# A hybrid attention step on one core: keys and queries of mixer A projected and normed during mixer B, index dots block by block

## The reference

```python
xn = rms_norm(x, norm_g)
h = einsum('btd,de->bte', xn, w_in)
qa, ka, va, ua, qi, ki, wi, qb, kb, vb, ub, ga, gb = split(h)
qa, ka = rope(rms_norm(qa, q_norm_g)), rope(rms_norm(ka, k_norm_g))   # per head
qi, ki = rope(qi), rope(rms_norm(ki, idx_k_norm_g))
# mixer A: index scores, top 128 keys (72 for the samples), softmax over them
dots  = einsum('bqhd,bsd->bqhs', qi, ki) * 64 ** -0.5
score = einsum('bqhs,bqh->bqs', relu(dots), wi)      # masked to the admissible keys
oa = softmax(qa . ka[top_k(score)] * 64 ** -0.5) . va[top_k(score)]
# mixer B: stick breaking, strictly causal
z  = einsum('bqhd,bshd->bhqs', qb, kb) * 64 ** -0.5
ob = (exp(log_sigmoid(z) + sum of log_sigmoid(-z) behind the key)) . vb
y  = x + (sigmoid(ga) * (oa * silu(ua)) @ w_a_out + sigmoid(gb) * (ob * silu(ub)) @ w_b_out) @ w_o
```

## Time and profile before

| | us |
|---|---|
| median of the runs | 573.23 |
| time of the profiled execution | 572.14 |
| its span, first to last instruction | 570.4 |
| PE busy in the span | 539.1 |
| DVE, ACT, POOL busy | 323.1, 222.4, 76.4 |
| mean granted TensorE clock | 0.973 of full speed |

### The profile page before, as it was taken

How to read it: one execution, slowest core, us unless ns; L and a number is a source line. 1 busy time by engine, 2 the same in 40 slices (tenths; PEclk the granted TensorE clock), 3 DMA queues, 4 the chain that set the end, 5 groups by cost and what they waited for, 6 DMA issues and landing times.

```text
span 570.4 us, 10220 instructions
## 1 busy us (share of the span) xinstructions
PE 539.1 (95%) x4344; PEld 511.8 (90%) x4344; DVE 323.1 (57%) x650; ACT 222.4 (39%) x354; POOL 76.4 (13%) x87
## 2 busy tenths in 40 slices
PE   4999699999999999989969799999999999999998
PEld 3889699999999999979969788898899999999997
DVE  5805647788987886734763456663245433456331
ACT  7614645215445456423403666643413323123110
POOL 4313000001342222160450000000000000000000
PEclk9999989999999999987979899999899999999999
DMA  8611202541102220240422005021033222227311
GB/s 329 239 74 38 85 1 74 183 160 64 51 37 76 75 75 1 75 148 1 153 74 75 2 1 180 22 75 38 1 111 111 75 60 90 75 94 280 140 49 50
DMA packets 15214, 50.45 MB, mean 88 GB/s; under 512 B 2400, under 2 KB 5856, under 8 KB 11584
## 3 DMA queue, kind: packets, MB, share of 16 engines
q1 hardware_dynamic: 15168, 49.79, 24.7%
HBM read 42.82 MB, written 6.82 MB: 87 GB/s over the span
## 4 chain that ended last, share of the span: by engine, by line
PE 86%; DVE 5%; POOL 3%; ACT 3%; issue 2%; DMA 1%; SPq 0%; ACTq 0%; DVEq 0%
PE PS L506 34%; PE PS L723 13%; PE PS L784 9%; PE PS L766 8%; PE PS L460 4%; PE PS L638 4%; PE PS L617 3%; PE PS L492 3%; POOL nrs L1584 2%; PE PS L561 2%; PE PS L593 2%; PE PS L701 2%; ACT whi L830 1%; PE PS L454 1%; DVE wlo L1111 1%
## 5 line engine op out<-in xcount | busy, mean ns | idle before, releaser
L506 PE MATMUL PS<-xhi,whi 128*128 128x272 f32 x320 | 94.9, 297 | 5.7 <-DVE q_flat L1216 5.3
L1111 DVE TENSOR_TENSOR wlo<-raw,whi 128x2048 fp32r<-128x2048 f32 (+1 forms) x36 | 74.4, 2068 | 36.0 <-ACT whi L830 35.9
L506 PE MATMUL PS<-xlo,whi 128*128 128x272 f32 x320 | 93.2, 291 | 0.0
L506 PE MATMUL PS<-xhi,wlo 128*128 128x272 f32 x320 | 92.7, 290 | 0.0
L830 ACT ACTIVATE whi<-raw 128x2048 fp32r<-128x2048 f32 (+1 forms) x36 | 61.7, 1718 | 76.8 <-PE PS L723 33.7
L506 PE MATMUL PS<-whi,xhi 128*128 128x256 f32 x256 | 77.3, 302 | 3.9 <-DVE oT L1304 3.3
L506 PE MATMUL PS<-wlo,xhi 128*128 128x256 f32 x256 | 75.3, 294 | 0.0
L506 PE MATMUL PS<-whi,xlo 128*128 128x256 f32 x256 | 74.7, 292 | 0.0
L506 PEld LDWEIGHTS PS<-xhi,whi 128*128 128x128 f32 x320 | 60.9, 190 | 9.3 <-DVE q_flat L1216 5.6
L506 PEld LDWEIGHTS PS<-xhi,wlo 128*128 128x128 f32 x320 | 61.0, 191 | 0.0
L506 PEld LDWEIGHTS PS<-xlo,whi 128*128 128x128 f32 x320 | 60.9, 190 | 0.0
(11 more groups left out here) (204 smaller groups left out, 1135.2 us busy)
## 6 DMA issues: line engine op xcount, KB each, us to landing
raw<-in_w_units SPq DMA_DIRECT2D x28, 1024.0 KB, 4.9
stage<-in_x_kw_qi SPq DMA_DIRECT2D x8, 564.0 KB, 7.2
raw<-in_w_mixes SPq DMA_DIRECT2D x8, 512.0 KB, 3.5
res<-in_x_kw_qi SPq DMA_DIRECT2D x1, 2176.0 KB, 8.0
out<-res SPq DMA_DIRECT2D x16, 136.0 KB, 1.7
out<-vals SPq DMA_DIRECT2D x2, 1024.0 KB, 5.4
out<-kT SPq DMA_DIRECT2D x1, 1088.0 KB, 6.5
out<-tm SPq DMA_DIRECT2D x1, 1024.0 KB, 4.3
```

The costliest lines, as they stand in the source:

```text
L506: mm = pe.matmul(out, lhsT, rhs, start=(k == 0), stop=(k == 23))
L1111: dve.tensor_tensor(wlo[:, uu % 2, 0:n], raw[:, uu % 2, 0:n], whi[:, uu % 2, 0:n].bitcast(F32), ALU.subtract).then_inc(w_lo, 1)
```

## The change

- `UNITS`: `ub0` goes ahead of `kb0`; `ka0` and `ka1` go ahead of `ub1`. The loads on SP follow, and the store of A's new keys moves ahead of the load of `ua1`.
- Four groups of `vb1` stand ahead of the dots. The dots go block by block (3, 2, 1, "s"), eight heads each, with a group after every fourth dot. From block 2 on DVE makes a round of top-k on block 3 after every second dot. `topk_half` now takes the two blocks that are furthest behind.
- Nine groups (`PRE_B`) instead of seven stand between the dots and mixer B.
- In mixer B, ACT squares the keys (from slot 11) and the queries (from slot 25) tile by tile. DVE makes the mean a slot later, POOL the root of that tile (128x8) a further slot later (`roots`), and scale, gain and rotation have slots of their own in `norms`: keys 19 to 24, queries 33 to 38.
- After B, the slots go on: two groups, the key transposes, seven groups, the query transposes, two groups (`POST_B`).

The diff, cut to its core:

```diff
-UNITS = [(n, KIND[n[:2]]) for n in ("vb0", "vb1", "kb1", "kb0", "qb0", "qb1", "ub0", "ub1", "ka0", "ka1", "qa0", "qa1",
+UNITS = [(n, KIND[n[:2]]) for n in ("vb0", "vb1", "kb1", "ub0", "kb0", "qb0", "qb1", "ka0", "ka1", "ub1", "qa0", "qa1",
                                     "ua0", "ua1", "va0", "va1")]
 
-DOT_FILL = groups_of("vb1")[2:] + groups_of("kb1") + groups_of("kb0")[:1]
-B_FILL = groups_of("qb1", "ub0", "ub1", "ka0", "ka1", "qa0", "qa1")
+DOT_FILL = groups_of("vb1")[4:] + groups_of("kb1") + groups_of("ub0")[:3]
+DOTS_PER_FILL = 4
+PRE_B = groups_of("ub0")[3:] + groups_of("kb0", "qb0")
 B_SLOTS = 2 * (N_STEPS + 2)
+B_FILL = groups_of("qb1", "ka0", "ka1", "ub1", "qa0", "qa1", "ua0")[:B_SLOTS]
+POST_B = groups_of("ua0")[2:] + groups_of("ua1", "va0")
 A_FILL = groups_of("va1", "gate0", "gate1")
 
-K_SUM_STEPS = (11, 12, 13)
+K_SLOT, Q_SLOT = 11, 25
...
-    if _g in B_FILL[:B_SLOTS]:
+    if _g in B_FILL:
...
-DOTS = [(h, b) for h in range(H) for b in SCORED]
+DOTS = [(h, b) for b in SCORED for h in range(H)]
...
@@ @block.sync
-            load_unit("kb0")
+            load_unit("ub0")
...
-            load_unit("qb0")
+            load_unit("kb0")
...
-            load_unit("qb1")
+            load_unit("qb0")
             sp.wait_ge(dot_done, len(DOTS))
             sp.dma_start(kT[:, :, NT:KEYS], cache_b_k).then_inc(cache_bk_in, 16)
+            load_unit("qb1")
...
-            load_unit("ub0")
+            load_unit("ka0")
             group_out_wait(sp, LAST_GROUP[U["kb0"]])
             sp.dma_start(new_b_k_fm, kT[:, :, 0:NT]).then_inc(st_kb, 16)
-            for name in ("ub1", "ka0", "ka1", "qa0", "qa1", "ua0", "ua1", "va0"):
+            for name in ("ka1", "ub1", "qa0", "qa1", "ua0"):
                 load_unit(name)
+            sp.wait_ge(k_rows, 1)
+            sp.dma_start(rows_p(new_a_k_p), tm[:, 0:4, W:2 * W]).then_inc(st_ka, 16)
+            sp.dma_start(rows_s(new_a_k_s), tm[0:DEC, 4, W:2 * W]).then_inc(st_ka, 16)
+            load_unit("ua1")
+            load_unit("va0")
             sp.wait_ge(pv_done, N_STEPS)
             sp.wait_ge(st_kb, 16)
             sp.dma_start(kT[:, :, SEQ:SEQ + PAST], cache_a_k).then_inc(cache_ak_in, 16)
             sp.dma_start(vals[:, 4:6, :], rows_p(cache_a_v)).then_inc(cache_av_in, 16)
             load_unit("va1")
-            sp.wait_ge(k_rows, 1)
-            sp.dma_start(rows_p(new_a_k_p), tm[:, 0:4, W:2 * W]).then_inc(st_ka, 16)
-            sp.dma_start(rows_s(new_a_k_s), tm[0:DEC, 4, W:2 * W]).then_inc(st_ka, 16)
...
@@ @block.tensor
-            for g in groups_of("vb1")[:2]:
+            for g in groups_of("vb1")[:4]:
                 group(g)
             pe.wait_ge(item_lo, len(I_ITEMS) + 1)
...
+            for n, (h, b) in enumerate(DOTS):
+                if n >= 6:
+                    pe.wait_ge(relu_done, n - 5)
+                m, q, k0 = (DEC, iqS[:, h, :], SEQ) if b == "s" else (P, iqT[:, h, P * b:P * b + P], 0)
+                for c in range(2):
+                    mm = pe.matmul(ps[0:m, n % 6, 0:n_keys(b)], q, ikT[:, c, k0:k0 + n_keys(b)],
+                                   start=(c == 0), stop=(c == 1))
+                mm.then_inc(dot_done, 1)
+                if n % DOTS_PER_FILL == DOTS_PER_FILL - 1:
+                    group(DOT_FILL[n // DOTS_PER_FILL])
+            for g in PRE_B:
                 group(g)
...
             pe.wait_ge(pv_out, 5)
-            for g in B_FILL[B_SLOTS:]:
-                group(g)
-            unit("ua0")
             pe.wait_ge(k_rows, 1)
             pe.wait_ge(at_out, N_STEPS)
             for bank in (2, 3):
                 group_out_wait(pe, max(g for g in B_FILL if BANK[g] == bank))
+            for g in POST_B[:2]:
+                group(g)
             for n in K_ITEMS:
                 item(n)
-            unit("ua1")
-            unit("va0")
+            for g in POST_B[2:-2]:
+                group(g)
             pe.wait_ge(q_rows, 1)
             for n in Q_ITEMS:
                 item(n)
+            for g in POST_B[-2:]:
+                group(g)
...
@@ @block.scalar
+            for g in groups_of("vb1")[:4]:
+                filled(g)
+            for n, (h, b) in enumerate(DOTS):
+                act.wait_ge(dot_done, n + 1)
+                if n >= 4:
+                    act.wait_ge(acc_done, n - 3)
+                m = DEC if b == "s" else P
+                act.activation(relus[0:m, n % 4, 0:n_keys(b)], ps[0:m, n % 6, 0:n_keys(b)], ACT.Relu,
+                               scale=HD ** -0.5).then_inc(relu_done, 1)
+                if n % DOTS_PER_FILL == DOTS_PER_FILL - 1:
+                    filled(DOT_FILL[n // DOTS_PER_FILL])
+            for g in PRE_B:
+                filled(g)
...
-            def key_squares(t):
+            def square_tile(t, c, k, name):
 
                 n = TILES[t][1]
-                if t == 0:
-                    group_out_wait(act, LAST_GROUP[U["ka1"]])
+                group_out_wait(act, FIRST_GROUP[U[name]] + t)
                 if t == 4:
-                    act.wait_ge(sample_rows, sample_units("ka1"))
-                if t >= 1:
-                    act.wait_ge(k_summed, t)
-                act.activation(square[0:n, :], tm[0:n, t, W:2 * W], ACT.Square).then_inc(k_square, 1)
+                    act.wait_ge(sample_rows, sample_units(name))
+                if k >= 1:
+                    act.wait_ge(summed_up, k)
+                act.activation(square[0:n, :], tm[0:n, t, c:c + W], ACT.Square).then_inc(squared, 1)
+
+            def squares(slot):
+                if K_SLOT <= slot < K_SLOT + 5:
+                    square_tile(slot - K_SLOT, W, slot - K_SLOT, "ka1")
+                if Q_SLOT <= slot < Q_SLOT + 5:
+                    square_tile(slot - Q_SLOT, 0, 5 + slot - Q_SLOT, "qa1")
...
             for n in K_ITEMS:
                 item(n)
-            for g in groups_of("ua1", "va0"):
+            for g in POST_B[2:-2]:
                 filled(g)
             for n in Q_ITEMS:
                 item(n)
+            for g in POST_B[-2:]:
+                filled(g)
...
@@ @block.vector
+            def topk_half():
+
+                todo = sorted(SCORED, key=lambda b: rounds_done[b] - ROUNDS[b])
+                topk(*todo[:2])
...
+            filling = [None]
+
+            def fill(g):
+
+                filled(g)
+                if filling[0] is not None:
+                    unit_next(filling[0])
+                filling[0] = g
+
+            for g in groups_of("vb1")[:4]:
+                fill(g)
+            for n, (h, b) in enumerate(DOTS):
+                dve.wait_ge(relu_done, n + 1)
+                m, t = (DEC, 4) if b == "s" else (P, b)
+                r, w = relus[0:m, n % 4, 0:n_keys(b)], wis[0:m, t, h:h + 1]
+                if h == 0:
+                    dve.tensor_scalar(scores(b), r, w, None, ALU.mult).then_inc(acc_done, 1)
+                else:
+                    dve.wait_ge(acc_done, n)
+                    dve.scalar_tensor_tensor(scores(b), r, w, scores(b), ALU.mult, ALU.add).then_inc(acc_done, 1)
+                if h == H - 1:
+                    dve.wait_ge(acc_done, n + 1)
+                    if b == 3:
+                        link(dve.memset(scores(3)[0:CHUNK, n_keys(3) - CHUNK:n_keys(3)], NEG))
+                if n % DOTS_PER_FILL == DOTS_PER_FILL - 1:
+                    fill(DOT_FILL[n // DOTS_PER_FILL])
+                if b != 3 and n % 2:
+                    topk(3)
+
+            for b in (2, 1):
+                dve.memset(scores(b)[0:CHUNK, n_keys(b) - CHUNK:n_keys(b)], NEG)
+            link(dve.memset(bias[:, QOFF[0]:QOFF[0] + P], 0.0))
+            link(dve.memset(bias[0:CHUNK, QOFF[0] + CHUNK:QOFF[0] + P], NEG))
+
+            for g in PRE_B:
+                fill(g)
                 topk_half()
...
+            def mean_squares(t, k):
+
                 n = TILES[t][1]
-                dve.wait_ge(k_square, t + 1)
-                dve.tensor_reduce(nss[0:n, t, :], square[0:n, :].rearrange("p (h d) -> p h d", h=H), AX.X,
-                                  ALU.add).then_inc(k_summed, 1)
+                dve.wait_ge(squared, k + 1)
+                if k >= 5:
+                    dve.wait_ge(rooted, 5)
+                link(dve.tensor_reduce(nss[0:n, t, :], square[0:n, :].rearrange("p (h d) -> p h d", h=H), AX.X, ALU.add))
+                dve.tensor_scalar(nss[0:n, t, :], nss[0:n, t, :], 1.0 / HD, EPS, ALU.mult, ALU.add).then_inc(summed_up, 1)
...
+            def norms(slot):
+
+                if K_SLOT + 1 <= slot < K_SLOT + 6:
+                    mean_squares(slot - K_SLOT - 1, slot - K_SLOT - 1)
+                if Q_SLOT + 1 <= slot < Q_SLOT + 6:
+                    mean_squares(slot - Q_SLOT - 1, slot - Q_SLOT + 4)
+                if slot in (K_SLOT + 8, K_SLOT + 9):
+                    dve.wait_ge(rooted, 5)
+                    norm_scale(W, slot - K_SLOT - 8)
+                if slot in (K_SLOT + 10, K_SLOT + 11):
```

(129 more changed lines are left out.)

100 lines of the change are left out of this document (10 added, 90 removed).

## The result

The changed kernel takes 575.4 us (median of 12 runs, 573.6 to 578.6), the kernel before 572.8 in the same comparison (12 runs): ratio 1.0056, 95% interval 1.0039 to 1.0072. The forecast was 569.7. In the profiled executions the span, from the first to the last instruction, grew from 570.4 to 574.0 us. Marks in PE's work split it into five stretches; "neutral" is the old stretch with the work that moved in or out.

What follows compares the result with a forecast made beforehand. PE bounds the kernel, so only its idle and low-clock time can change. Saved 8.0, less 3.8 and 0.7, is 3.5 us: 572.1 becomes 568.6, the median 1.1 above, 569.7 us; own range 565.5 to 574, wider range 561.5 to 577.5.

Steps and rivals of the forecast that it cites:

- mixer B: Mixer B to step 13: no PE idle time, DVE's load falls, ACT waits as before; cost 0.
- POOL's cover: Mixer B: POOL's weights, two pows and a silu fit in a step of 8.8 us; if not, 1 to 2 us.
- Stage 1: Up to mixer B's first step: DVE becomes the bound, z(0) at 144.4, a loss of 3.8 us plus 0.7 for low clock.
- the chained accumulations: Dots in block order: each accumulation waits for the one just ahead, taken as 0.12 us more each.
- The tail: B's step 13 to mixer A's second `va1` group: 4.5 us of idle time and 3.5 of low clock saved, 8.0 us.
- The low clock: Tail: of 7.1 us lost at the low clock, half, 3.6 us, was kept.
- `pv_out`: Tail: PE waits 2.1 us for DVE's evacuation of slot 29, ACT's square, a sum and `weighed`.
- `q_rows`: Tail: 10 us of DVE's work in a row against three token groups, 8.6: 1.4 us idle.
- Rival 1: Waits in DVE's queue cost nothing and PE sets stage 1 too: 561 to 564.5 us; chance 0.24.
- Rival 2: New idle times still drop the clock; the tail gives only 4.5 us and stage 1 takes it: 573.2 us; chance 0.20.
- Rival 3: In the dots, `ub0`'s Sigmoids and the Relus throw out each other's table: 575.5 us, or 578; chance 0.14.

Runs made afterwards that it cites:

- the w_low experiments: The changed kernel with POOL's silu on 8 of 272 columns, 571.72 us; then also step 7's product L1584 on 8 columns per head, 573.93 us; single runs.
- the one with the thin silu: The changed kernel with POOL multiplying only 8 of the 272 columns in each silu; a single run, 571.72 us.
- The last kernel: The changed kernel with slots 9 and 23, two squares buffers, gate0 inside mixer A, early Exp, no top-k rounds among the dots: 548.75 us, 0.9585 to before.

## Why the prediction was wrong

**The step that failed** is mixer B: "ACT waits for DVE in `square_tile` as it did before", "Cost 0; if POOL's or SP's cover failed, a step would slip by 1 to 2 us". It cost 4.7 us: 3.1 of wait at L641 and some 1.6 of low clock behind it, which two other executions with the same wait don't have. I had added up DVE's and POOL's load per slot, and it fits: DVE is busy 92.4 of 111.8 us. But ACT's square is a wait for one DVE instruction, and behind it in ACT's queue stands the copy that PE needs next. What matters is the longest thing ahead of the sum in the slot, 3.52 + 0.67 + 0.17 us, and not the mean. In the prediction's own terms, I didn't name what is queued behind the waiting instruction. In the kernel before, the squares came at slots 22 to 26, and mixer B had no such wait. The second buffer shows the mechanism, and the w_low experiments its parts. POOL's cover, which the sentence names as the risk, was not what failed: its pow of 128x8 took 1.64 us, as forecast, but its product made w_low 1.24 us longer.

**Stage 1** was right in mechanism: DVE is the bound (17.1 of 18 us busy at 104 to 122), and the chained accumulations are slower. Four of 512 columns take 3.32 us, 0.83 each; in the kernel before, one of 512 is followed after 0.67, so the wait costs 0.16 where I took 0.12.

```profile
81.76 3.32 DVE L1282 SCALAR_TENSOR_TENSOR bias<-wk,wis,bias 128x512 f32<-128x512 f32 x4 [3.15 <-ACT wk L939]
```

In size, predicted from the first matmul to z(0) were 137.6 us with the low clock. Six of the seven profiled executions with this stage 1 have 137.4 to 138.3, and the change's own has 139.3: there the clock was at 0.72 over 122 to 128, and at 1.00 in the six others. So 1.7 of the miss is this execution's low clock. One sum is off: 143.1 and 1.0 are 144.1, not 144.4. What the rounds cost, 10 us of z(0) (137.4 to 127.6), I had put down only as part of DVE's sum; I didn't ask what they would cost in mixer B, where PE has no wait on DVE but the sums: with two squares buffers, nothing.

**The tail** was right in mechanism, each wait where I had put it, but that 7.7 came so near to 8.0 is luck in part. Idle times of 2.1, 1.4, 0.9 and 3.9 us were predicted, 2.9, 1.8, 1.0 and 4.0 measured, so they save 3.1 us and not 4.5. The low clock made up for it: with 2.4 us left of 7.1 it saved some 4.7, where I had kept half as a guess. `pv_out` was the least exact, since the same square stands in front of it: 1.9 with two buffers. For `q_rows` the terms add up to 9.6 before any overlap, not 10, so they give 1.0 and not the 1.4 written.

**The rivals.** Rival 1 (waits cost nothing, PE sets stage 1) is false, z(0) came at 147.2 and not before 141. Rival 2 (573.2) gave a time near the measured one, but by the wrong way: the tail gained all I forecast. Rival 3 had the right sign for a wrong reason: ACT's trace after has a single table load in the dots, 1.28 us at 102.85, and none among the Relus behind it. The range held the time; the direction was wrong. Rival 1's premise is false too, as a waited-on accumulation costs 0.16 us more; in the kernel without the rounds that doesn't reach z(0).

The ledger of the two profiled executions closes: 3.5 us faster were forecast, 3.6 slower came, and 7.1 = 4.7 (mixer B) + 1.7 (stage 1) + 0.4 (start) + 0.3 (tail). The 1.7, the 0.4 and the low clock in the 4.7 come in some executions and not in others; by the medians the miss is 5.7 us.

What stays open is which idle times drop the clock. With the same wait of 3.1 at L641, mixer B from z(0) to its product for the samples is 118.5 us long in the change and in the kernel with gate0 one step later. It is 116.9, at clock 1.00 throughout, in the kernel with gate0 inside A, whose code there is the same, and in the one with the thin silu. The spread of the runs goes along with the clock: the change's fastest run, 573.57 us, has a mean clock of 0.988, its slowest, 578.59, one of 0.979. The last kernel spreads over 2 us in place of 5.

## What to carry to other kernels

When a wait is added to an in-order engine, look at the instruction behind it and at the longest thing ahead of the releasing one, slot by slot; a mean load that fits says nothing. With a single buffer between two busy engines, one queue stops with the other: a second buffer cost 512 columns of a tile that lay free and gave 6.4 us. Move a step to where its engine waits for something else anyway: the same w_high and w_low gave nothing one step later, and 6.9 us two steps on with the table's load ahead.

## What the hardware showed

The text ahead of the prediction says that the engines meet only at semaphores. DVE and POOL meet elsewhere too: DVE's w_low (two inputs in SBUF) and POOL's products don't run side by side. Whichever starts second waits for the end of the first and then takes its usual time: w_low 3.52 us behind an L1584 of 1.54 and 3.98 behind one of 2.00, in place of 2.28; in turn a silu of 0.76 takes 2.28 when it starts 0.6 us into w_low, and even one of 8 columns 2.26. DVE's evacuation L1213, with one of its two inputs in PSUM, takes 0.41 us and L1584, which starts inside it, its usual 1.54. The Trainium skill says this on its page "SBUF — State Buffer", section "SBUF: two separate sides": a DVE instruction with two inputs in SBUF and a GpSimd one that reads SBUF take the port pair that they share as an exclusive lock for the whole instruction, and the one that comes second blocks. The experiments agree. It could have put the 1.24 us on w_low in slot 14; that the copy stands behind the square would still have had to be seen.
